# A gated scan's output gates, copied out of PSUM ahead of the next weight tile's rounding

## What is computed

```
    (a_q, a_k, a_v, a_g, g_q, g_k, g_v, g_af, g_ab, g_g,
     s_u, s_v, s_g, m_a, m_g, m_s) = jnp.split(h @ p['w_in'], pts, axis=-1)
...
    ol_f, _ = gla_scan(qlg, klg, vlg, gfl, s_f)
    ol_b, _ = gla_scan(flip(qlg), flip(klg), flip(vlg), flip(gbl), s_b)
    y_gla = gla_finish(ol_f + flip(ol_b), p['gla_o_norm'], x.dtype) * jax.nn.silu(g_g)
...
        m = (jax.nn.sigmoid(ga) * (ya @ p['w_br_attn'])
             + jax.nn.sigmoid(gg) * (yg @ p['w_br_gla'])
             + jax.nn.sigmoid(gs) * (ys @ p['w_br_sgu']))
```

## Time and profile before

| | |
|---|---|
| median of 3 runs | 3389.44 us (3384.95 to 3391.86) |
| the profiled execution | 3384.89 us |
| its span, first to last instruction | 3383.1 us |
| TensorE busy | 3103.9 us, 92% |
| VectorE busy | 1915.5 us, 57% |
| ScalarE busy | 1179.9 us, 35% |
| GpSimd busy | 210.6 us, 6% |
| granted TensorE clock, mean | 0.964 |

### The profile page before, as it was taken

The page is one execution under the profiler, slowest core; times in us unless marked ns, Lnnn a source line. Parts: engine busy times, 40 slices in busy tenths (PEclk is TensorE's granted clock), DMA queues, the critical chain, the costliest instruction groups (busy, mean ns, idle before and its releaser), DMA issues.

```text
span 3383.1 us, 43105 instructions
## 1 busy us (share of the span) xinstructions
PE 3103.9 (92%) x17878; PEld 2575.9 (76%) x17878; DVE 1915.5 (57%) x2796; ACT 1179.9 (35%) x1795; POOL 210.6 (6%) x138
## 2 busy tenths in 40 slices
PE   7998899999999788999989899988999998898898
PEld 6787778888887666788877788875788776776677
DVE  7776555656434674788543543557353645456655
ACT  4224341212223453322343333325222543433432
POOL 0003100000010000000000320000000203100000
PEclk9998899999999999999989999999999999999999
DMA  5554123333321002555431122200313222230123
GB/s 211 158 181 137 44 75 125 125 125 125 102 67 63 14 1 75 172 189 186 126 87 62 59 83 80 93 26 1 98 63 135 74 79 75 88 116 26 66 94 125
DMA packets 100091, 323.92 MB, mean 96 GB/s; under 512 B 14310, under 2 KB 20326, under 8 KB 98744
## 3 DMA queue, kind: packets, MB, share of 16 engines
q1 hardware_dynamic: 89812, 291.29, 26.6%
q10 hardware_dynamic: 10084, 29.87, 2.4%
HBM read 301.46 MB, written 19.66 MB: 95 GB/s over the span
## 4 chain that ended last, share of the span: by engine, by line
PE 78%; DVE 9%; ACT 7%; issue 4%; DMA 1%; POOL 1%; ACTq 0%; SPq 0%; DVEq 0%; POOLq 0%
PE PS L391 77%; ACT whi L198 1%; PE PS L394 1%; ACT Pq L1319 1%; DVE STs L1356 1%; DVE STq L1356 1%; DVE wlo L212 1%; ACT Ps L1319 1%; DMA Ht<-in_hT 1%; ACT nt L641 0%; ACT FS L1746 0%; POOL rows L2589 0%; POOL rows L2587 0%; DVE JUNK L544 0%; DVE mH L1158 0%
## 5 line engine op out<-in xcount | busy, mean ns | idle before, releaser
L391 PE MATMUL PS<-U,whi 128*128 128x512 f32 (+1 forms) x4992 | 1072.3, 364 | 77.5 <-DVE U L671 21.3
L391 PEld LDWEIGHTS PS<-U,whi 128*128 128x128 f32 x4992 | 844.9, 193 | 248.9 <-issue 42.9
L212 DVE TENSOR_TENSOR wlo<-stage,whi 128x1024 fp32r<-128x1024 f32 x339 | 427.1, 1262 | 966.8 <-ACT whi L198 966.3
L198 ACT ACTIVATE whi<-stage 128x1024 fp32r<-128x1024 f32 x339 | 357.8, 1057 | 1348.3 <-PE PS L391 1277.3
L391 PE MATMUL PS<-U,wlo 128*128 128x512 f32 (+1 forms) x2496 | 552.5, 355 | 0.0
L391 PE MATMUL PS<-Y,whi 128*128 128x512 f32 (+1 forms) x2240 | 506.1, 362 | 13.6 <-DVE Y L2236 4.5
L391 PEld LDWEIGHTS PS<-U,wlo 128*128 128x128 f32 x2496 | 419.4, 189 | 73.7
L391 PEld LDWEIGHTS PS<-Y,whi 128*128 128x128 f32 x2240 | 383.2, 190 | 87.7 <-issue 7.2
L391 PE MATMUL PS<-whi,U 128*128 128x512 f32 (+2 forms) x1152 | 323.1, 368 | 8.4 <-ACT g1qk L1773 1.9
L391 PE MATMUL PS<-Y,wlo 128*128 128x512 f32 (+1 forms) x1120 | 283.5, 360 | 0.0
L391 PEld LDWEIGHTS PS<-whi,U 128*128 128x128 f32 x1152 | 205.9, 189 | 51.0 <-issue 6.2
(11 more groups left out here) (432 smaller groups left out, 3114.0 us busy)
## 6 DMA issues: line engine op xcount, KB each, us to landing
stage<-in_w SPq DMA_DIRECT2D x128, 512.0 KB, 4.0
stage<-in_ada SPq DMA_DIRECT2D x80, 512.0 KB, 3.7
stage<-in_adb SPq DMA_DIRECT2D x48, 512.0 KB, 3.8
stage<-in_p_mg SPq DMA_DIRECT2D x16, 512.0 KB, 3.7
stage<-in_p_ma SPq DMA_DIRECT2D x16, 512.0 KB, 3.7
stage<-in_p_ms SPq DMA_DIRECT2D x16, 512.0 KB, 3.7
stage<-in_wo SPq DMA_DIRECT2D x16, 512.0 KB, 3.6
GS<-FS ACTq DMA_DIRECT2D x20, 384.0 KB
```

The lines of the kernel that those rows point to most:

```text
L198: act.activation(self.parts[r % n][0], self.stage[i % len(self.stage)], ACT.Copy).then_inc(*self.S.up("w_hi", i))
L212: dve.tensor_tensor(lo, self.stage[i % len(self.stage)], hi.bitcast(F32), ALU.subtract).then_inc(*self.S.up("w_lo", i))
L391: return pe.matmul(o, l, r, start=start, stop=stop_, skip_group_check=True)
```

## The change

It touches the eight output gates. `act_step` first copies the projection from PSUM into `FS` (new event `g_raw`), then rounds the next weight tile, then takes the sigmoid from `FS`. `dve_step` multiplies by `FS`, no longer by PSUM. The next projection waits for `g_raw` in place of `g_gate`. Since `FS` now serves both kinds of tile, two waits are added on ScalarE: the raw copy waits until the spill of the tile before it has landed (`BEHIND` holds its number), and the next branch gate's copy waits for `g_gate`.

```diff
@@ scan_steps
     for place in places:
         if place[0] == "lv" and place[2] in (2, 4):
             tiles[place] = ("p_gg", 2 * place[1] + place[2] // 4, None)
+            behind[tiles[place][1]] = len(gates) - 1
...
-STEPS, EARLY = scan_steps()
+STEPS, EARLY, BEHIND = scan_steps()
@@ pe_step
-            pe_proj(pe, T(name + str(L), j), xU, L == 0, ("g_gate", L, j) if n is None else ("fill", L, n))
+            pe_proj(pe, T(name + str(L), j), xU, L == 0, ("g_raw", L, j) if n is None else ("fill", L, n))
@@ act_step
-            W.hi(act, i)
-            act.wait_ge(*at("w_used", i))
             if n is None:
-                act.activation(GL[L].G[j // 2][j % 2][:, 0:N], B.of(i)[:, 0:N], ACT.Sigmoid).then_inc(*up("g_sig", L, j))
+                act.wait_ge(*at("w_used", i))
+                act.wait_ge(*at("spill", L, BEHIND[j]))
+                act.activation(FS[:, 0:N], B.of(i)[:, 0:N], ACT.Copy).then_inc(*up("g_raw", L, j))
+                W.hi(act, i)
+                act.wait_ge(*at("g_raw", L, j))
+                act.activation(GL[L].G[j // 2][j % 2][:, 0:N], FS[:, 0:N], ACT.Sigmoid).then_inc(*up("g_sig", L, j))
             else:
+                W.hi(act, i)
+                act.wait_ge(*at("w_used", i))
                 if n or L:
                     act.wait_ge(*(at("spill", L, n - 1) if n else at("spill", 0, len(EARLY) - 1)))
+                for k, last in BEHIND.items():
+                    if last == n - 1:
+                        act.wait_ge(*at("g_gate", L, k))
                 act.activation(FS[:, 0:N], B.of(i)[:, 0:N], ACT.Copy).then_inc(*up("fill", L, n))
@@ dve_step
-                dve.tensor_tensor(y, y, B.of(i)[:, 0:N], ALU.mult).then_inc(*up("g_gate", L, j))
+                dve.tensor_tensor(y, y, FS[:, 0:N], ALU.mult).then_inc(*up("g_gate", L, j))
```

More of the change, by code:

```diff
@@ L50 @@
     "y_hi": ("f_hi", "s_yhi", "g_yhi", "q_yhi", "v_yhi"), "y_lo": ("f_lo", "s_ylo", "g_ylo", "q_ylo", "v_y"),
-    "h_new": ("res", "b_add", "e_r", "h_final"), "evicted": ("m_qk", "s_qk", "q_z", "fill", "g_qk", "g_af", "v_x"),
+    "h_new": ("res", "b_add", "e_r", "h_final"), "evicted": ("m_qk", "s_qk", "q_z", "fill", "g_raw", "g_qk", "g_af", "v_x"),
     "modulated": ("n_mul", "u_mod"), "gain": ("n_gain", "u_gain"), "rows_act": ("m_va", "g_va"),
@@ L229, in scan_steps @@
     early = [(tag, j) for tag in "gas" for j in range(8)]
-    tiles, gates = {}, {}
+    tiles, gates, behind = {}, {}, {}
     for place in places:
@@ L238, in scan_steps @@
             tiles[place] = ("p_m" + tag, j, n)
-    return tiles, gates
-STEPS, EARLY = scan_steps()
+    return tiles, gates, behind
+STEPS, EARLY, BEHIND = scan_steps()
 def weight_plan():
```

## The result

The changed kernel takes **3370.53 us** (median of 4, 3366.87 to 3372.88), the kernel before 3390.65 us (median of 4). The ratio is 0.9944 with an interval of 0.9931 to 0.9958: 0.6% faster, 20 us. Forecast were 3356 us and a range up to 3369; the time lies 1.5 us above it. The profiled execution took 3370.91 us with a span of 3369.1 us.

What follows compares the result with a forecast made beforehand. TensorE bounds the kernel, with 78% of the span; 22.7 us of waiting and 10.6 us of clock at eight output gates make 33.3 us, so 3389.4 - 33.3 = 3356 us, range 3348 to 3369 us.

Steps and rivals of the forecast that it cites:

- What bounds it, and the wait's parts: Eight output gates: TensorE waits 22.1 us for the multiply; in layer 0 2.78 us over rounding, table load, sigmoid, multiply.
- The copy is ahead of the level's matmuls: Output gates: the PSUM copy ends before TensorE needs the banks, 0.53 us ahead in layer 0, 0.29 us in layer 1.
- The clock of the first groups: First 16 matmuls behind output gates: slow groups of 5.53 us return to 3.99 us, 10.6 us of clock in all.
- The sum for the scans: Both layers' output gates: 17.6 us in layer 0 plus 15.7 us in layer 1, 33.3 us in all.
- What the change adds is hidden: Output gates: eight ScalarE copies, 5.5 us, and the new waits cost TensorE nothing; cover left 3.1 and 1.2 us.
- The collision with POOL: Layer 1's multiply, now reading two SBUF tiles, may meet POOL's pair: at most 1.26 us, 0.1 us of the sum.
- Rival 1: Clock still falls in places, so only the waits, 22.7 us, are saved: 3367 us, chance 0.07.

Runs made afterwards that it cites:

- the filler experiment: Changed kernel plus eight useless 512-column matmuls in the wait ahead of layer 1's V projection: 3356.95 us; the kernel before with the same matmuls: 3382.59 us.
- the kernels with the V projection at the high clock: Changed kernel plus eight useless matmuls, ahead of layer 1's second attention projection (3355.10 us) or in the wait ahead of its V projection (3356.95 us).

## Why the prediction was wrong

- **What bounds it, and the wait's parts:** right. TensorE's 22.1 us at the eight gates are gone, and the branch gates' waits stay at 8.7 us.
- **The copy is ahead of the level's matmuls:** right in both layers; 1.54 and 1.09 us from level to projection.
- **The clock of the first groups:** right at the gates, all eight now take 4.00 us. One group elsewhere in layer 0's scan took over a fall (5.52 us).
- **The sum for the scans:** 33.3 us forecast, 15.9 + 15.5 = 31.4 us measured in the traces; 1.5 us of the difference is that one group.
- **What the change adds is hidden:** right. No level waited for a late factor, and no raw copy for a spill. The collision with POOL came about, and was harmless: beside POOL's L2004 the low part took 1.78 us for 1.23, POOL's pair 2.59 us for 2.30, the multiply 1.12 us for 0.95. The Trainium skill ("SBUF — State Buffer", on engine ports) says that a VectorE instruction with two SBUF inputs and a GpSimd instruction that reads SBUF shut each other out for whole instructions. The trace agrees that both get longer, with 0.55 us on L212, which started 0.13 us behind POOL's; how much of it is waiting the trace does not show.
- **The step that failed** is the sum's closing, "In all 33.3 us ... From the profiled execution's 3384.9 us this gives 3351.6 us". It took all work outside of the eight gates to be as long as before. With the change layer 1's V projection, which it does not touch, ran at the low clock and took 29.1 us for 16.3; the filler experiment shows that the cost is this clock, and not a wait elsewhere. Rival 1 said that the clock may fall "in places" but priced only the rows beside the gates, at 10.6 us of gain not had; no rival had a stretch that was fast before and becomes slow. With 12.8 us for it the sum would have been 3369 us. That rival 1's 3367 us lies near the measured time is chance, since its mechanism, slow groups at the gates, did not occur.
- **What is luck:** the kernels with the V projection at the high clock stand at 3355.1 and 3356.95 us, where the forecast of 3356 us stood, but the kernel before stood at 3386 us beside them and not at 3389.4. The gain there is 31 and 29 us, and 25.6 us with the filler in both kernels, for 33.3 forecast. Of the 7.7 us between, 1.9 us is what the scans' sum lacks by the first two traces; where the rest lies stays open.

## What to carry to other kernels

When a saving moves long stretches of TensorE work in time, look for stretches of narrow matmuls behind a wait. Price them at the low clock once, as a rival of the forecast. Compare the two traces at fixed points of the program, and fill the wait ahead of such a stretch, in both kernels, before judging the change. And when a table load stands ahead of an activation, look at what stands ahead of the load: put the instruction that waits behind both, and the load can run during the wait, as it did here (2.4 us less of TensorE's wait for 1.0 expected).

## What the runs showed of the hardware

A stretch of 144 matmuls of 128 columns, without a gap, that TensorE entered at the high clock fell to the low one 2 us after its start and stayed there to its end, at a busy share of 29.08 in 29.10 us. It did so in five of nine traces without a filler, 0.8 to 2.1 us after its start. Matmuls of 512 columns behind longer waits (2.75 us) fell too in seven of eight places of the kernel before, but were soon back: the stretch of 5.4 us around the first 16 had a mean of 0.68, and the next 4.8 us had 1.00. The Trainium skill ("TensorE: Matmul & The Clock Gate", on oscillation in real kernels) tells of a matmul kernel with M = 128 that falls back at every tile, each time behind a wait for a transfer. This trace differs: the one wait, of 1.84 us and for ScalarE, lies ahead of the stretch, and none lies inside the 29 us. Eight matmuls of 512 columns in the wait ahead kept the whole stretch at 16.3 us. So did eight that stood 35 us ahead (six of six runs by their times), where four did not (one of five runs by its time).
